# Mixer of a hybrid trunk: sums of squares as two fp32r products, the low half made on VectorE, head 1's sum placed behind its slot's plane products

## What is computed

```
o_a = chunk_gated_linear_attention(q, 1 - forget, v, log(forget))     # one head: (512, 128)
o_a = rmsnorm(o_a, hg_norm) * silu(hg)
rmsnorm(x, g) = x * rsqrt(mean(x * x, axis=-1) + 1e-6) * g
out = concatenate(heads) @ w_out
```

## Time and profile before

| | us |
|---|---|
| median of 3 runs | 1189.23 |
| lowest and highest | 1188.87, 1189.93 |
| the profiled execution, its own time | 1189.59 |
| its span, from the first to the last instruction | 1187.9 |
| PE busy | 1162.4 (98%) |
| PE weight loads busy | 961.4 (81%) |
| DVE busy | 798.3 (67%) |
| ACT busy | 624.3 (53%) |
| POOL busy | 127.2 (11%) |
| chain that ended last | PE 89%, DVE 5%, ACT 4% |

### The profile page before, as it was taken

The page is one execution under the profiler, slowest core; times in us unless marked ns, Lnnn a source line. Parts: engine busy times, 40 slices in busy tenths (PEclk is TensorE's granted clock), DMA queues, the critical chain, the costliest instruction groups (busy, mean ns, idle before and its releaser), DMA issues.

```text
span 1187.9 us, 16254 instructions
## 1 busy us (share of the span) xinstructions
PE 1162.4 (98%) x5835; PEld 961.4 (81%) x5835; DVE 798.3 (67%) x1190; ACT 624.3 (53%) x1161; POOL 127.2 (11%) x129
## 2 busy tenths in 40 slices
PE   8999999999999999999999999999999999999997
PEld 6788788887978888888888877778978888888886
DVE  5456767775577677668477368765577687668464
ACT  6554465545655445545535756655655445545431
POOL 2321323310121111120000000100000000000000
PEclk9999999999999999999999999999999999999999
DMA  5322112233432332232232231203423332231321
GB/s 164 89 76 67 55 54 55 71 121 119 143 106 90 106 123 81 93 110 71 89 107 81 69 89 56 80 19 93 155 102 94 103 126 77 92 115 54 104 75 71
DMA packets 87522, 108.20 MB, mean 91 GB/s; under 512 B 9202, under 2 KB 48227, under 8 KB 87460
## 3 DMA queue, kind: packets, MB, share of 16 engines
q1 hardware_dynamic: 85716, 101.87, 27.2%
q0 software_dynamic: 1744, 5.51, 1.5%
HBM read 104.22 MB, written 2.10 MB: 90 GB/s over the span
## 4 chain that ended last, share of the span: by engine, by line
PE 89%; DVE 5%; ACT 4%; issue 2%; DMA 1%; DVEq 0%; SPq 0%; ACTq 0%
PE bank L1870 23%; PE bank L1872 23%; PE bank L1871 23%; PE pp L1871 3%; PE pp L1872 3%; PE pp L1870 3%; PE pp L2024 2%; PE po L2362 2%; PE pp L1927 1%; DVE w_lo L620 1%; ACT w_hi L611 1%; PE po L2035 1%; PE pp L2014 1%; PE pp L2343 1%; PE po L2038 1%
## 5 line engine op out<-in xcount | busy, mean ns | idle before, releaser
L1870 PE MATMUL bank<-h_lo,w_hi 128*128 128x512 f32 (+3 forms) x748 | 287.7, 385 | 4.5 <-DVE w_lo L620 2.1
L1872 PE MATMUL bank<-h_hi,w_hi 128*128 128x512 f32 (+3 forms) x748 | 284.5, 380 | 0.0
L1871 PE MATMUL bank<-h_hi,w_lo 128*128 128x512 f32 (+3 forms) x748 | 284.3, 380 | 0.0
L1870 PEld LDWEIGHTS bank<-h_lo,w_hi 128*128 128x128 f32 x748 | 140.7, 188 | 33.8 <-issue 4.1
L1872 PEld LDWEIGHTS bank<-h_hi,w_hi 128*128 128x128 f32 x748 | 140.7, 188 | 26.4
L1871 PEld LDWEIGHTS bank<-h_hi,w_lo 128*128 128x128 f32 x748 | 140.8, 188 | 24.9
L1870 PE MATMUL bank<-wx,a_hl 128*128 128x512 f32 x320 | 125.5, 392 | 0.0
L609 ACT CAST wx<-raw 128x1024 fp32r<-128x1024 f32 x72 | 74.6, 1049 | 95.9 <-DVE raw L1565 64.7
L1872 PE MATMUL bank<-wx,a_hl 128*128 128x512 f32 x320 | 124.7, 390 | 0.0
L1871 PE MATMUL bank<-wx,a_hl 128*128 128x512 f32 x320 | 124.6, 389 | 0.0
L1576 DVE TENSOR_TENSOR y<-y,bank 128x512 f32<-128x512 f32 x80 | 54.8, 685 | 87.5 <-PE bank L1872 87.3
(11 more groups left out here) (365 smaller groups left out, 2164.4 us busy)
## 6 DMA issues: line engine op xcount, KB each, us to landing
stage<-in_mlp_w SPq DMA_DIRECT2D x66, 512.0 KB, 3.8
raw<-in_mlp_w SPq DMA_DIRECT2D x50, 512.0 KB, 3.5
stage<-in_ev_w_in SPq DMA_DIRECT2D x28, 512.0 KB, 3.8
spare<-in_mlp_w SPq DMA_DIRECT2D x12, 512.0 KB, 4.9
stage<-in_ev_w_out SPq DMA_DIRECT2D x8, 512.0 KB, 3.6
stage<-in_od_w_out SPq DMA_DIRECT2D x8, 512.0 KB, 3.5
stage<-in_od_w_in SPq DMA_DIRECT2D x10, 256.0 KB, 3.0
x_tok<-in_x SPq DMA_DIRECT2D x4, 512.0 KB, 5.3
```

Source lines behind the costliest of these rows:

```text
L1870: nc.tensor.matmul(dst, wh, xl_, start=first, stop=False)
L1871: nc.tensor.matmul(dst, wl, xh, start=False, stop=False)
L1872: return nc.tensor.matmul(dst, wh, xh, start=False, stop=last)
```

## The change

The squares are made in the split format and summed by two fp32r products in place of one fp32 product. ACT squares `po` a second time, into `sq_hi` (fp32r). A new DVE step, `square_low`, subtracts it from the fp32 square and gives `sq_lo` (fp32r). PE adds ones times `sq_lo` and ones times `sq_hi`. The semaphore `o_sq` now counts three steps a head. `ones` becomes an fp32r tensor. `sq_hi` lies over `rinv[:, 0]` and `sq_lo` over `sq[:, 0]` in SBUF; `sq` and `rinv` move behind `tok`, with the total unchanged.

`square_low` stands on DVE in the slot behind that of the square, between the evacuation and the gating, for all heads but one. For head 1, whose sum is in the very next slot, it stands at the end of the square's own slot (21), behind the copies; and its sum on PE moves behind the plane products of slot 22.

```diff
-        ones = sb("ones", [P, P])
+        ones = sb("ones", [P, P], F32R)
...
-        sq = sb("sq", [P, 2, T])
         tmp = sb("tmp", [P, 2, T])
-        rinv = sb("rinv", [P, 2, T])
         tok = sb("tok", [P, 16, NT])
+        with ExitStack() as sums:
+            sq = sb("sq", [P, 2, T], F32, sums)
+            rinv = sb("rinv", [P, 2, T], F32, sums)
+        with ExitStack() as sums:
+            sq_lo = sb("sq_lo", [P, T], F32R, sums)
+            sb("beside_sums", [P, T], F32, sums)
+            sq_hi = sb("sq_hi", [P, T], F32R, sums)
+        sb("under", [P, 4, T])
...
                 nc.scalar.activation(sq[:, 0, :], po[:, :], ACT.Square).then_inc(o_sq, 1)
+                nc.scalar.activation(sq_hi[:, :], po[:, :], ACT.Square).then_inc(o_sq, 1)
                 nc.scalar.activation(sq[:, 1, :], po[:, :], ACT.Copy).then_inc(o_read, 1)
...
+            def square_low(o):
+                dve.wait_ge(o_sq, 3 * o + 2)
+                nc.vector.tensor_tensor(sq_lo[:, :], sq[:, 0, :], sq_hi[:, :].bitcast(F32), ALU.subtract).then_inc(o_sq, 1)
...
                     split_low(dve, EO + SPLIT - 1)
+                for o in SQUARES[i - 1] if i >= 1 else ():
+                    if o not in SUMS[i]:
+                        square_low(o)
                 for o in MIXES[i]:
                     head_gate(o)
...
                     group(o, c)
+                for o in SQUARES[i]:
+                    if o in SUMS[i + 1]:
+                        square_low(o)
                 if i in EXT_SLOTS:
...
             def head_sum(o):
-                pe.wait_ge(o_sq, o + 1)
+                pe.wait_ge(o_sq, 3 * o + 3)
                 pe.wait_ge(o_read, o + 1)
-                nc.tensor.matmul(po[:, :], ones[:, :], sq[:, 0, :], start=True, stop=True).then_inc(o_sum, 1)
+                nc.tensor.matmul(po[:, :], ones[:, :], sq_lo[:, :], start=True, stop=False)
+                nc.tensor.matmul(po[:, :], ones[:, :], sq_hi[:, :], start=False, stop=True).then_inc(o_sum, 1)
...
+                late = [o for o in SUMS[i] if o in SQUARES[i - 1]]
                 for o in SUMS[i]:
-                    head_sum(o)
+                    if o not in late:
+                        head_sum(o)
                 for lead, step in groups:
...
+                for o in late:
+                    head_sum(o)
```

More of the change, by code:

```diff
@@ L770, in _ @@
         def _(pool):
-            nc.gpsimd.memset(ones[:, :], 1.0).then_inc(consts_ready, 1)
+            nc.gpsimd.memset(ones[:, :].bitcast(F32), 1.0).then_inc(consts_ready, 1)
             nc.gpsimd.memset(eps[:, :], EPS).then_inc(consts_ready, 1)
@@ L1440, in cumulate @@
                     s = slice(c * P, (c + 1) * P)
-                    ins = nc.vector.tensor_tensor_scan(b_sb[:, s], ones[:, :], t_f[:, s], 0.0, ALU.mult, ALU.add)
+                    ins = nc.vector.tensor_tensor_scan(b_sb[:, s], ones[:, :].bitcast(F32), t_f[:, s], 0.0, ALU.mult, ALU.add)
                 ins.then_inc(b_ready, 1)
+            def square_low(o):
+                dve.wait_ge(o_sq, 3 * o + 2)
+                nc.vector.tensor_tensor(sq_lo[:, :], sq[:, 0, :], sq_hi[:, :].bitcast(F32), ALU.subtract).then_inc(o_sq, 1)
             def head_gate(o):
@@ L1932, in _ @@
             for h, g_bank in ((0, po), (1, misc)):
-                nc.tensor.matmul(g_bank[:, :], ones[0:1, :], grow[:, h * T:(h + 1) * T], start=True,
+                nc.tensor.matmul(g_bank[:, :], ones[0:1, :].bitcast(F32), grow[:, h * T:(h + 1) * T], start=True,
                                  stop=True).then_inc(gain_ready, 1)
```

## The result

| | us | of before, same chips |
|---|---|---|
| changed kernel, 22 runs | 1190.95 median, 1188.41 to 1191.94 | 1189.16 |
| ratio | 1.0012 (95%: 1.0006 to 1.0017) | |
| profiled execution, its own time | 1188.41 | 1189.59 |
| its span | 1186.7 | 1187.9 |

So the change costs 1.4 us by the ratio, 1.8 by the medians. The forecast was 1190.0 with +0.8. Oddly, the profiled execution is faster than that of before. The runs say why one has to be careful with it: they fall into two groups, 8 at 1188.4 to 1189.5 and 14 at 1190.5 to 1191.9, and the profiled one is the fastest of the lower group. The forecast lies between the two: the lower group is centred on 1189.2, no higher than before, the upper one on 1191.3. The profile shows the mechanics of the change; what the upper group has, it can't show.

The account below looks back on a forecast made before the run. PE was taken as nearly full in the mixer, but in step with DVE at three places. Head by head, 0.61 + 1.09 - 0.24 - 0.40 + 0.49 + 0.03 - 0.80 = +0.8 us, so 1190.0, range 1186.6 to 1192.0.

Parts of the forecast that it names:

- head 0: Slot 19: `square_low(0)` delays a DVE chain PE already waits for, and PE's saving is lost in the wait; +0.61 us.
- head 1: PE idles 1.5 us at the sum for `square_low(1)`, with slot 23's projection queued behind; +1.09 us.
- head 2: PE waits 0.16 us at the sum for the low half, so only 0.24 us is gained.
- head 3: `square_low(3)` falls where DVE and ACT are idle around slot 27's evacuation; full gain of 0.40 us.
- head 4: ACT's second square delays slot 30's chain by 0.49 us; the sum's 0.40 saving is swallowed in PE's wait; +0.49.
- heads 5 to 7: Head 5 keeps a loss of 0.03 us; heads 6 and 7 hide the step and gain 0.80 together.
- plane 6: Plane 6 of head 5: PE's wait for a copy grows from 1.36 to 2.25 us.
- head 6's outputs: PE waits 0.43 us for a DVE copy made 0.49 later, with PE 0.40 earlier.
- low halves are hidden everywhere: Rival, chance 0.13: only PE's saving shows at all eight heads, 3.2 us off, 1186.0.
- the sum saves nothing: Rival, chance 0.04: an fp32r sum costs what the fp32 sum does; about +2.7 us, 1191.9.
- POOL: Rival, chance 0.10: POOL's decay holds up `square_low(1)`, head 1's sum comes 0.84 us later; +1.6, 1190.9.
- the clock: Rival, chance 0.06: the clock falls to 1.2 GHz behind the waits at heads 1 and 4, 1.5 us each; 1193.0.

Follow-up runs that it names:

- the second execution of before: The kernel before the change, unchanged, profiled once more: 1188.31 us, against 1189.59 in the first profile of the same kernel.
- the repetition: The changed kernel run again with no edit: 1191.51 us median of 11 runs, ratio 1.0016 to the kernel before.

## Why the prediction was right in its mechanism and short in its size

**The sum by heads, like with like.** After's profile and the second execution of before both have the early start and the short subtractions. Laid over each other at head 0's outputs (106.61 and 107.27, so 0.66 is added), the changed kernel is later by 0.23 at the end of slot 20, then 1.40 at head 2's outputs (146.93 - 146.19 + 0.66), 1.34 behind head 2's sum (156.72 - 156.04), 0.91 behind head 3, 1.37 at plane 6 (212.95 - 212.24), 0.88 at the end of the mixer (282.23 - 282.01). The product that the prediction wanted near 282.6 in place of 281.84 stands at 280.74 in after and at 280.51 in the second execution of before, 0.89 later with the 0.66.

| | predicted | measured |
|---|---|---|
| head 0 | +0.61 | +0.23, +0.61 with the long subtractions |
| head 1 | +1.09 | +1.17 |
| head 2 | -0.24 | -0.06 |
| head 3 | -0.40 | -0.43 |
| head 4 | +0.49 | +0.46 |
| heads 5 to 7 | -0.77 | -0.49 |
| sum | +0.78 | +0.88 |

**Right:** the price and pitch of every new operation; PE's idle of 1.60 at head 1's sum (1.5 predicted), 2.25 at plane 6 (2.25), 0.35 at head 6's outputs (0.43); the swallowed saving of head 4; the way that the shift passes on whole, 904.47 and 904.59 us behind the mixer. The medians of the kernels with few heads fit it, with intervals of some 1.1 us to either side: heads 3, 6 and 7 gain 1.2 and 1.5 (1.20), head 1 costs 1.2 (1.09). That low halves are hidden everywhere and that the sum saves nothing are both out. POOL didn't hold `square_low`: 0.69 at the most.

**Mis-sized, small.** Head 0 has two prices, since the chain that I followed from 118.62 is tight only where the third subtraction is long; the kernel with head 1's low half earlier drew the long one and lost 140.63 - 108.17 = 32.46 against 31.85, the 0.61. Head 2 waits 0.22 and not 0.16, and its first product behind the wait takes 0.34 and not 0.23. Head 5 lost 0.10 (0.03 predicted), head 7 gained 0.41 (0.40), but head 6 only 0.18: at the first product behind its outputs PE's load stands still again, for a `y` of DVE, a wait that isn't in the trace of the second execution of before. Both small waits in after's timeline of weight loads:

```profile
155.73 0.19 PEld L2064 LDWEIGHTS po<-sq_lo,ones 128*128 128x128 f32 x1 [0.48 <-DVE sq_lo L1453]
...
254.78 0.19 PEld L1887 LDWEIGHTS bank<-w_lo,a_hl 128*128 128x128 f32 x1 [0.15 <-DVE y L1434]
```


**Mis-sized, and the reason for the rest: the clock.** I had the mechanism, both its places and its price (1.5 a fall; measured 1.63, 7.63 - 6.03 = 1.60, and 8.06 to 8.10 less 6.48, 1.6), and gave it 0.06, on the evidence that the products go on at full rate behind 1.36 and 1.56 us. The row that I took for a fall, the half rate behind the idle of 1.40 us, was none: the rate was half ahead of the idle as well. The failing step is the sentence that it decides only if a wait of 2.25 us is past what keeps the clock. There is no such point in the runs. The same 2.25 was followed by the fall in the profiles of three kernels and passed at full clock in two, after's and the repetition's; the same 1.60 was followed by it in two and passed in three; 0.83 was followed by it once, and 0.84 passed. It is a share of the executions, not a case that is true or false. In the changed kernel and its repetition 24 of 33 runs are in the upper group. I also had it as two falls or none; no profile of the changed kernel or its parts shows more than one in the mixer, and +0.8 with one fall makes +2.4 over before, about where the upper group lies (+2.1). The profiled run of the repetition closes the account: 1191.51 - 1188.31 = 3.20, of which 0.88 is the sum by heads, 1.63 the fall, and 0.67 the late start (107.94 for 107.27).

One thing the fall alone doesn't give: the groups are 2.1 apart and not 1.6, and the lower one lies at before's median and not 0.9 over it. Lower runs that started early and upper ones that started late would do this. The profiles point that way: of the nine with 1.6 us or more at head 1 or 1.78 or more at plane 6, five of the six with the late start have a fall and one of the three with the early start. That is argued from few profiles; no run fixes the start.

So the median lies 1.0 over the forecast because of one fall in some seven of ten executions. The wait alone, as the profile's view of waits puts it, was priced right, and its consequence on the clock was left to a rival.

What stays open is what decides in one execution. Rows show what PE did before: at plane 6 it had come from 16 plane products and 6 of the states, at head 0's place from outputs that start 0.42 us a pair; at the end of the mixer the same 1.6 us stood behind a run of 512-column products, and no fall came there in any of the fourteen profiles. At one and the same place the length counts: at plane 6 the fall stands behind 1.4 us in none of seven profiles, behind 1.8 in one of two, and behind 2.25 in three of five. The Trainium skill, "TensorE: Matmul & The Clock Gate", section "A second HAM failure mode: psum-queue depth-cycling", tells of a kernel in which frequent short idle times between groups of matmuls made the clock swing. This case's traces agree in so far as short idle times were enough, 0.83 and 1.60 us; here a single one was followed by a single fall, and how often they come was not tried. That the density ahead of the wait is what counts was only argued here; no run varied it alone.

## What to carry to other kernels

A wait that is new on a full TensorE has two prices: its length, and a chance of a stretch at half clock, which may be larger; keep a low-part step only where its engine is idle beside it (heads 3, 6 and 7 here, 1187.5, the lowest median of a kernel with whole sums, though within 0.2% of before), and count what each head brings before changing all eight. When the times of one kernel fall in groups, take a profile from each before explaining the median. Lay two profiles over each other behind the last place at which executions of the unchanged kernel differ, or the luck of the draw is larger than the effect.

## What the hardware showed beyond expectation

- A stretch at the level of 1.2 GHz followed waits of 0.83, 1.60, 1.83 and 2.25 us in some executions, and 0.84, 1.60, 1.78 and 2.25 us were passed at full clock in others. It lasted some 3.4 us and cost 1.3 to 1.63 us.
- TensorE began each execution at half rate. In seven profiles its products started at the full rate by 13 us of the span, in the other seven only from 16 to 17 us on, of before and changed kernels alike. Head 0's outputs came at 106.61 to 107.44 in the first and at 107.94 to 108.17 in the second.
- The three DVE subtractions of 128x512 at slot 19, with the same POOL decay beside them, took 1.85 to 1.91 us in eight profiles and 2.77 to 2.79 in six, of before and changed kernels alike. The Trainium skill, "SBUF — State Buffer", section "SBUF: two separate sides", has VectorE stand still while GpSimd holds the shared port pair; the two lengths agree with one waiting for that lock and not always meeting it.
- The first fp32r product behind a wait or behind fp32 products starts the next one 0.34 us later (140.90, 141.24), those behind another fp32r product 0.23.
